# First layer's gates: the modulation weights of each branch consumed in two groups of four, each behind the first half of a gate product

## The chip, the cores and the metric

The kernel runs on one core of one Trainium2 chip. The metric is the device time of one execution in microseconds. Three runs of the kernel before took 3114.62, 3114.74 and 3118.58 us, a median of 3114.74 us. All data are float32.

In this text TensorE is PE, VectorE is DVE, ScalarE is ACT, GpSimd is POOL and SyncE is SP. PE reads its operands from the on-chip memory SBUF and sums in PSUM, which has eight banks of 128 partitions by 512 floats.

## The reference, cut to what matters

The program is a two-layer trunk (attention of three kinds, a Fourier branch, a mixture of 16 experts) followed by a second block of two more layers. What the change touches is the part of the first layer in which the four branches are gated and merged, and the six vectors by which the layer shifts and scales its tokens ("modulation"):

```
def trunk_layer(h_lat, h_ctx, c, c_ctx, w_mod, b_mod, w_in, ...):
    m_lat = (jax.nn.silu(c) @ w_mod + b_mod)[:, None, :]
    m_ctx = jax.nn.silu(c_ctx) @ w_mod + b_mod
    sh1, sc1, g1, sh2, sc2, g2 = jnp.split(m_lat, N_MOD, -1)
    ...
    u_lat = h_lat * (1.0 + sc1) + sh1
    y_lat, y_ctx = token_mixers(u_lat, u_ctx, w_in, ...)
    h_lat = layer_norm(DN_ALPHA * h_lat + g1 * y_lat, ln1_g, ln1_b)

def merge_branches(branches, gate_logits, w_branch, w_out):
    gates = jax.nn.sigmoid(gate_logits)
    merged = gates[..., :D_MODEL] * (branches[0] @ w_branch[0])
    for i in range(1, N_BRANCH):
        merged = merged + gates[..., i * D_MODEL:(i + 1) * D_MODEL] * (branches[i] @ w_branch[i])
    return merged @ w_out
```

The width is 1024; there are 256 latent and 256 context tokens, so 512 columns in the first layer. The gate logits are 4096 of the columns of `u @ w_in`, 1024 for each branch. `w_mod` is 1024 x 6144 for each of the two layers: 12288 columns for a product with only two vectors, `c` and `c_ctx`.

## The kernel before

**The weight stream.** Every large weight is cut into units of 1024 x 256 floats, 1 MB each. The host lays them in one list in the order in which PE uses them (`weight_stream`). SBUF holds a ring of eight units (`ring`). SP refills it (L489): for each unit it waits until the counter `units_used` says that the unit eight places earlier was consumed, and then issues one 1 MB transfer. PE takes units with `unit()`, which waits until the unit has landed (`loaded[n % RING]`). So PE can run at most eight units ahead of a transfer, and a unit is released in list order.

**The modulation product.** `w_mod` of both layers is 48 units in six sets of eight. Two sets are used before the part in question; the other four are used in the first layer's gate stage, one set for each branch. `modulation_rows` multiplies four units at a time: `cs` (the activated `c` and `c_ctx`, padded to 32 columns) is the stationary operand, and each of the four units writes its own 32 partitions of a PSUM bank, so that four units make 32 matmuls of 32 x 256 (L844). Two such groups fill the banks `wb` and `wb + 1`. DVE copies both to SBUF (L2039, L2041, the two tiles of `mrow`), PE transposes them (`modulation_columns`, L852), and DVE adds the bias and writes the vectors `mod` (`columns_of`, L1888).

**The gate stage** (`mix_branches`, on PE, ACT and DVE each). Sixteen chunks of 256 columns run in four slots of four; a slot is a branch, in the order of `ORDER`. In each chunk of the first layer PE issues: the first half of the gate product (L870: 8 matmuls of 128 x 512 into bank `gb`), one step of attention, the second half of the gate product (L870, bank `gb + 1`), another step of attention, and the branch product (L895: 4 matmuls into banks `wb` and `wb + 1`). An attention step `attend(i)` is: transpose the probabilities of pair i (`turn`, L806) in two halves, mix the values of pair i-1 between them (L819), and compute the scores of pair i+1 (L785, with a mask product L790 or L793 for two of the kinds). There are 24 pairs, so the attention ends with chunk 11; chunk 12 mixes the last pair.

On DVE a chunk is: the softmax of pair 2·chunk (L1991 to L2003, with ACT's exponential L1527 in between), then `merge` of the chunk before (L2023 in the first slot; L2026 and L2027 in the others), which frees the banks `wb` and `wb + 1` and counts `merged_step`, then in the first chunk of a slot the work on the modulation rows and columns, then the copy of mixed values (L2012) and the softmax of pair 2·chunk+1. ACT takes the gate's tanh (L1557) and copies the transposed probabilities (L1541).

**In the first chunk of each slot** PE does the whole modulation product before anything else: it waits for `merged_step` (both banks `wb` are still being read by the merge), runs the two groups of four units, and only then takes the gate unit, which is the ninth unit of the list there. After the first half of the gate product it waits for `rows_kept` and transposes the columns.

Below, "the first half of the gate product" is the L870 group with j = 0.

## Time and profile before

| | us |
|---|---|
| median of 3 runs | 3114.74 |
| profiled execution, its own time | 3111.43 |
| its span, first to last instruction | 3109.6 |
| PE busy | 2841.2 |
| DVE busy | 858.0 |
| ACT busy | 347.8 |
| mean DMA rate over the span | 220 GB/s |

The profile is of one execution. A row of the timeline gives where a run of equal instructions starts, how long it lasts, how many there are (a float32 matmul shows as two records, so "x16" is eight matmuls), and in brackets how long the engine had stood idle and what ended that. The gate stage of the first layer lies between 160 and 567 us. The granted clock (PEclk) is the share of TensorE's full speed of 2.4 GHz that was granted: 1.00 is that level, 0.50 is 1.2 GHz throughout a stretch, and values between are stretches with both.

### The profile page before, as it was taken

What the parts mean: (1) busy time and instruction counts of PE and PEld (TensorE: products, weight loads), DVE (VectorE), ACT (ScalarE), POOL (GpSimd) and SP (SyncE); (2) the same over time, 40 slices, a digit from 0 to 9 for tenths busy, and PEclk for the clock granted to TensorE, in tenths of its full rate; (3) what the DMA queues carried; (4) which work ended last, traced back from release to release, by engine and by line L of the source; (5) the groups of instructions that cost most, each with busy time, mean ns of one, the idle gap of its engine ahead of it and who ended that gap; (6) DMA issues with size and microseconds to landing.
All of it is one profiled execution on the core that took longest, in us unless ns stands there. A gap on an engine that the chain in (4) does not pass through costs nothing.

```text
span 3109.6 us, 39609 instructions
## 1 busy us (share of the span) xinstructions
PE 2841.2 (91%) x16504; PEld 2025.8 (65%) x16504; DVE 858.0 (28%) x1787; ACT 347.8 (11%) x710; POOL 52.7 (2%) x92
## 2 busy tenths in 40 slices
PE   7999999998888889999977777899999999998998
PEld 3644444466666667788644343488788887887887
DVE  1322321152222233432311111278622202222201
ACT  0012220020000002121100000011211001011000
POOL 1000000000000001000000000000000000000000
PEclk9999999999999999999998999999999999999999
DMA  8434135149999993233599999933232443342441
GB/s 325 175 143 157 56 157 199 68 157 421 421 420 421 420 411 113 95 107 132 202 415 413 419 418 417 416 140 136 105 122 97 157 144 117 122 142 81 151 148 39
DMA packets 97660, 684.05 MB, mean 220 GB/s; under 512 B 11488, under 2 KB 12640, under 8 KB 16992
## 3 DMA queue, kind: packets, MB, share of 16 engines
q1 hardware_dynamic: 91488, 660.17, 53.7%
q0 software_dynamic: 6016, 21.50, 2.2%
q8 instruction: 135, 2.21, 0.3%
q14 instruction: 21, 0.17, 0.0%
HBM read 678.22 MB, written 3.41 MB: 219 GB/s over the span
## 4 chain that ended last, share of the span: by engine, by line
PE 75%; DMA 19%; DVE 2%; issue 1%; ACT 1%; SPq 1%; ACTq 0%; DVEq 0%
PE ps L605 29%; DMA ring<-units 19%; PE ps L870 11%; PE ps L1032 9%; PE ps L895 3%; PE ps L1337 2%; PE ps L1169 2%; PE ps L623 1%; PE ps L614 1%; PE ps L696 1%; PE ps L692 1%; PE ps L988 1%; PE ps L785 1%; PE ps L916 1%; PE ps L806 1%
## 5 line engine op out<-in xcount | busy, mean ns | idle before, releaser
L1032 PE MATMUL ps<-ring,arena 128*64 128x256 f32 (+1 forms) x4096 | 439.1, 418 | 134.5 <-DMA ring<-units 130.9
L605 PE MATMUL ps<-h,ring 128*128 128x256 f32 (+1 forms) x2176 | 502.6, 393 | 4.9 <-ACT h L1496 4.9
L605 PEld LDWEIGHTS ps<-h,ring 128*128 128x128 f32 x2176 | 413.3, 190 | 92.0 <-issue 37.8
L1032 PEld LDWEIGHTS ps<-ring,arena 128*64 128x64 f32 (+1 forms) x4096 | 287.0, 140 | 274.9 <-issue 187.9
L870 PE MATMUL ps<-u,ring 128*128 128x512 f32 (+1 forms) x1024 | 340.8, 489 | 6.3 <-DMA ring<-units 6.3
L605 PE MATMUL ps<-arena,ring 128*128 128x256 f32 x1408 | 306.6, 379 | 4.7 <-DVE arena L2290 3.4
L605 PEld LDWEIGHTS ps<-arena,ring 128*128 128x128 f32 x1408 | 267.3, 190 | 42.1 <-DVE arena L2290 4.2
L870 PEld LDWEIGHTS ps<-u,ring 128*128 128x128 f32 x1024 | 194.0, 191 | 142.1 <-issue 120.5
L1047 PE MATMUL ps<-ring,arena 128*32 128x256 f32 x2048 | 237.4, 383 | 37.5 <-DMA ring<-units 33.2
L1047 PEld LDWEIGHTS ps<-ring,arena 128*32 128x32 f32 x2048 | 118.0, 109 | 154.5 <-DMA ring<-units 64.7
L2203 DVE COPY u<-ps 32x512 f32<-32x512 f32 (+1 forms) x128 | 70.9, 554 | 245.6 <-PE ps L1032 244.3
L2333 DVE SCALAR_TENSOR_TENSOR arena<-arena,vec 128x256 f32<-128x256 f32 x240 | 97.1, 477 | 0.0
L2227 DVE SCALAR_TENSOR_TENSOR u<-h,ps 128x512 f32<-128x512 f32 x20 | 13.7, 687 | 299.2 <-PE ps L605 299.2
L895 PE MATMUL ps<-arena 128*128 128x512 f32 (+1 forms) x256 | 89.2, 491 | 0.6 <-DVE arena L2012 0.6
L605 PE MATMUL ps<-u,ring 128*128 128x512 f32 (+1 forms) x256 | 85.5, 489 | 2.8 <-DVE u L1851 2.7
L2195 DVE TENSOR_TENSOR arena<-arena,ps 128x256 f32<-128x256 f32 x48 | 20.2, 421 | 239.8 <-PE ps L1032 131.7
L1630 ACT ACTIVATE arena<-ps 128x256 f32<-128x256 f32 x48 | 18.4, 383 | 578.0 <-PE ps L1047 315.3
L2191 DVE SCALAR_TENSOR_TENSOR arena<-arena,ps 128x256 f32<-128x256 f32 x48 | 20.2, 421 | 226.8 <-ACT arena L1630 226.6
L1487 ACT ACTIVATE u<-u 128x512 f32<-128x512 f32 x24 | 14.5, 630 | 590.0 <-DVE u L1821 590.0
L1991 DVE TENSOR_REDUCE small<-ps 128x2 f32<-128x1024 f32 (+1 forms) x36 | 37.7, 1047 | 151.1 <-PE ps L785 76.9
L605 PEld LDWEIGHTS ps<-u,ring 128*128 128x128 f32 x256 | 47.7, 190 | 37.6 <-issue 31.1
L2288 DVE TENSOR_SCALAR arena<-ps 128x512 f32 x32 | 22.1, 692 | 175.6 <-PE ps L605 175.6
(331 smaller groups left out, 2604.8 us busy)
## 6 DMA issues: line engine op xcount, KB each, us to landing
ring<-units SPq DMA_DIRECT2D x624, 1024.0 KB, 12.5
arena<-quarters POOLq DMA_DIRECT2D x32, 256.0 KB, 2.9
h<-tokens SPq DMA_DIRECT2D x1, 2048.0 KB, 26.0
arena<-neighbours POOLq DMA_DIRECT2D x32, 64.0 KB, 5.7
arena<-tokens POOLq DMA_DIRECT2D x1, 2048.0 KB, 8.9
arena<-memory POOLq DMA_DIRECT2D x2, 1024.0 KB, 5.4
con<-constants SPq DMA_DIRECT2D x1, 1712.0 KB, 20.2
early_values<-arena POOLq DMA_DIRECT2D x6, 256.0 KB, 5.2
```

What stands on the lines that cost most here:

```text
L605: last = nc.tensor.matmul(ps[:, g + j, 0:n], w[:, kt, j * P:(j + 1) * P], rhs[:, q * KT + kt, 0:n], start=(q == 0 and kt == 0), stop=(q == ...
L614: last = nc.tensor.matmul(ps[:, g, 0:n], mean, x[:, kt, 0:n], start=(kt == 0), stop=(kt == KT - 1))
L623: last = nc.tensor.matmul(ps[:, g + 1, 0:n], mean, sq[:, kt, 0:n], start=(kt == 0), stop=(kt == KT - 1))
L870: last = nc.tensor.matmul(ps[:, gb + j, 0:T], w[:, kt, j * P:(j + 1) * P], u[:, kt, 0:T], start=(kt == 0), stop=(kt == KT - 1))
L895: last = nc.tensor.matmul(ps[:, wb + j, 0:T], quarter[done % 2][:, kt, j * P:(j + 1) * P], branch[:, 2 * br + kt, 0:T], start=(kt == 0), s ...
L1032: last = nc.tensor.matmul(ps[j * slots:(j + 1) * slots, bank, lo:lo + UC], lhsT[:, kt, 0:slots], w[j][:, kt, :], start=(kt == 0), stop=(kt ...
L1047: last = nc.tensor.matmul(ps[j % 4 * slots:(j % 4 + 1) * slots, banks[j // 4], 0:UC], xcur[:, kt, 0:slots], w[j][:, kt, :], start=(kt == 0 ...
L1169: last = nc.tensor.matmul(ps[:, g + j, 0:S], w[:, kt, j * P:(j + 1) * P], h[:, kt, 0:S], start=(kt == 0), stop=(kt == KT - 1))
L1337: last = nc.tensor.matmul(ps[:, outs[c], j * S:(j + 1) * S], w[:, kt, j * P:(j + 1) * P], mixin[:, q * KT + kt, :], start=(q == 1 and kt = ...
L1991: link(v.tensor_reduce(m, ps[:, sb_:sb_ + 2, lo:512], AX.X, ALU.max))
L2203: last = v.tensor_copy(y4[half][CAP * e4:CAP * (e4 + 1), st, :] .rearrange("p (a j n) -> p a j n", j=beside, n=UC)[:, :, j, :], src.rearra ...
L2333: ins = v.scalar_tensor_tensor(conv[:, t, :], src, k, conv[:, t, :], ALU.mult, ALU.add)
```

## The change

The units, the products and the tiles stay as they are; their order in the list and in the program changes, in the first layer only.

In the list, the eight modulation units of a slot and its first gate units stood as m0 to m7, g0, g1, g2, g3. They now stand as m0 to m3, g0, m4 to m7, g1, g2, g3.

On PE, chunks 0 and 1 of a slot take one group of four modulation units each, after the first half of their gate product (in chunk 0 of the stage also after the scores of pair 0) and before the attention step. The wait for `merged_step` stands before that group and no longer at the start of the slot. Each group uses bank `wb` alone. The transposes of the columns move from chunk 0 to chunk 2 of the slot, behind the first half of its gate product. The branch product of chunks 0 and 1 waits for its copy of the rows, that of chunk 2 for the columns.

On DVE the two row copies stand in chunks 0 and 1, each behind the merge of the chunk before, and `columns_of` stands in chunk 2. ACT computes what it did and counts units in the new order.

```diff
@@ weight_stream
         for b in range(4):
+            gates = w_in[7 + 4 * ORDER[b]:11 + 4 * ORDER[b]]
             if l == 0:
-                parts.append(w_mod[2 + b])
-            parts.append(w_in[7 + 4 * ORDER[b]:11 + 4 * ORDER[b]])
+                parts += [w_mod[2 + b][:4], gates[:1], w_mod[2 + b][4:], gates[1:]]
+            else:
+                parts.append(gates)
@@ PE, mix_branches
-                def modulation_rows(chunk):
+                def modulation_rows(chunk, first):
                     if chunk:
                         pe.wait_ge(merged_step, chunk)
                     else:
                         pe.wait_ge(products_taken, products - 2)
-                    for n in range(2):
-                        w = [unit() for _ in range(4)]
-                        for kt in range(KT):
-                            for q in range(4):
-                                last = nc.tensor.matmul(ps[32 * q:32 * (q + 1), wb + n, 0:UC], cs[:, kt, :], w[q][:, kt, :],
-                                                        start=(kt == 0), stop=(kt == KT - 1))
-                        last.then_inc(units_used, 4)
-
-                def modulation_columns(n):
-                    pe.wait_ge(rows_kept, n + 1)
+                    w = [unit_at(first + q) for q in range(4)]
+                    for kt in range(KT):
+                        for q in range(4):
+                            last = nc.tensor.matmul(ps[32 * q:32 * (q + 1), wb, 0:UC], cs[:, kt, :], w[q][:, kt, :],
+                                                    start=(kt == 0), stop=(kt == KT - 1))
+                    last.then_inc(units_used, 4)
+
+                def modulation_columns(chunk, n):
+                    pe.wait_ge(merged_step, chunk)
+                    pe.wait_ge(rows_kept, 2 * n + 2)
...
-                    if l == 0 and c == 0:
-                        modulation_rows(chunk)
+                    first = state["unit"]
+                    if l == 0 and c < 2:
+                        state["unit"] += 4
                     w = unit()
...
-                                if c == 0:
-                                    modulation_columns(slot)
+                                if c < 2:
+                                    modulation_rows(chunk, first)
+                                if c == 2:
+                                    modulation_columns(chunk, slot)
                                 attend(2 * chunk)
...
-                    if l == 0 and c == 0:
+                    if l == 0 and c < 2:
+                        pe.wait_ge(rows_kept, 2 * slot + c + 1)
+                    if l == 0 and c == 2:
                         pe.wait_ge(columns_kept, slot + 1)
@@ DVE, mix_branches
-                    if l == 0 and chunk % 4 == 0:
+                    if l == 0 and chunk % 4 < 2:
+                        dve.wait_ge(units_used, at(units_used, 4))
+                        v.tensor_copy(mrow[chunk % 4], ps[:, wb, 0:UC]).then_inc(rows_kept, 1)
+                    if l == 0 and chunk % 4 == 2:
                         n = chunk // 4
-                        dve.wait_ge(units_used, at(units_used, 4))
-                        v.tensor_copy(mrow[0], ps[:, wb, 0:UC])
-                        dve.wait_ge(units_used, at(units_used, 4))
-                        v.tensor_copy(mrow[1], ps[:, wb + 1, 0:UC]).then_inc(rows_kept, 1)
                         dve.wait_ge(rows_turned, n + 1)
```

**PE at the start of the stage, chunk 0.** In these rows L844 (L848 in the changed kernel) is the modulation product, L870 (L876) the gate product, L785 (L790) the scores, L852 the column transposes, L806 (L811) the probability transposes. Before:

```order
L844 MATMUL ps<-ring,cond 32x256 [waits unit_loaded_1,unit_loaded_0,unit_loaded_2,unit_loaded_7,products_taken]
L844 MATMUL ps<-ring,cond 32x256 x31
L844 MATMUL ps<-ring,cond 32x256 [waits unit_loaded_5,unit_loaded_6,unit_loaded_4,unit_loaded_3]
L844 MATMUL ps<-ring,cond 32x256 x31
L870 MATMUL ps<-u,ring 128x512 [waits products_taken,unit_loaded_7]
L870 MATMUL ps<-u,ring 128x512 x7
L785 MATMUL ps<-arena 128x512 [waits rotated,products_taken]
L785 MATMUL ps<-arena 128x512
L852 MATMUL ps<-con,arena 128x128 [waits modulation_rows_kept]
L852 MATMUL ps<-con,arena 128x128 x3
L806 MATMUL ps<-con,arena 128x128 [waits probs_ready,products_taken]
```

And in the changed kernel:

```order
L876 MATMUL ps<-u,ring 128x512 [waits products_taken,unit_loaded_3]
L876 MATMUL ps<-u,ring 128x512 x7
L790 MATMUL ps<-arena 128x512 [waits rotated,products_taken]
L790 MATMUL ps<-arena 128x512
L848 MATMUL ps<-ring,cond 32x256 [waits unit_loaded_1,unit_loaded_0,unit_loaded_2,unit_loaded_7,products_taken]
L848 MATMUL ps<-ring,cond 32x256 x31
L811 MATMUL ps<-con,arena 128x128 [waits probs_ready,products_taken]
L811 MATMUL ps<-con,arena 128x128 x3
```

The gate product and the scores moved ahead of the modulation product, of which one group of the two is left here, and the column transposes are gone from the chunk.

**PE at the start of the third slot, chunk 8** (the second and fourth slot read alike). L895 (L905) is the branch product of chunk 7. Before:

```order
L895 MATMUL ps<-arena 128x512 [waits merged_step,quarter_loaded_1]
L895 MATMUL ps<-arena 128x512 x3
L844 MATMUL ps<-ring,cond 32x256 [waits unit_loaded_1,unit_loaded_0,unit_loaded_2,unit_loaded_7,merged_step]
L844 MATMUL ps<-ring,cond 32x256 x31
L844 MATMUL ps<-ring,cond 32x256 [waits unit_loaded_5,unit_loaded_6,unit_loaded_4,unit_loaded_3]
L844 MATMUL ps<-ring,cond 32x256 x31
L870 MATMUL ps<-u,ring 128x512 [waits gate_kept,unit_loaded_7]
L870 MATMUL ps<-u,ring 128x512 x7
L852 MATMUL ps<-con,arena 128x128 [waits modulation_rows_kept]
```

And in the changed kernel:

```order
L905 MATMUL ps<-arena 128x512 [waits merged_step,quarter_loaded_1]
L905 MATMUL ps<-arena 128x512 x3
L876 MATMUL ps<-u,ring 128x512 [waits gate_kept,unit_loaded_3]
L876 MATMUL ps<-u,ring 128x512 x7
L848 MATMUL ps<-ring,cond 32x256 [waits unit_loaded_1,unit_loaded_0,unit_loaded_2,unit_loaded_7,merged_step]
L848 MATMUL ps<-ring,cond 32x256 x31
L811 MATMUL ps<-con,arena 128x128 [waits turned_kept,probs_ready]
```

The gate product now follows the branch product directly and takes the unit of ring place 3, the fifth of the slot, where it took place 7 once more, the ninth; the wait for the merge stands behind it.

**DVE in chunk 8.** L2036 and L2037 are the merge of chunk 7, L2048 the copy of the first group's rows, L2022 the copy of mixed values, L2001 the start of the next softmax, all in the changed kernel:

```order
L2036 SCALAR_TENSOR_TENSOR arena<-arena,ps 128x1024 [waits merged_step,gate_kept,branch_summed]
L2037 TENSOR_TENSOR h<-h,arena 128x1024 [waits dve_step]
L2048 COPY arena<-ps 128x256 [waits units_used]
L2022 COPY arena<-ps 128x2x128 [waits values_mixed]
L2001 TENSOR_REDUCE small<-ps 128x2 [waits scores_ready]
```

The second row copy, which followed the first directly (L2039, L2041), now stands in the same place of chunk 9, and the column work in that of chunk 10.

## Rows read from the trace of the kernel before

**Rows 1.** Page, section 1: busy time of PE and its share.
```profile
PE 2841.2 (91%) x16504; PEld 2025.8 (65%) x16504; DVE 858.0 (28%) x1787; ACT 347.8 (11%) x710; POOL 52.7 (2%) x92
```

**Rows 2.** Chain that ended last, 150 to 510 us: shares by line.
```profile
by line: PE ps L870 50.3%; PE ps L895 9.9%; PE ps L785 5.9%; DMA ring<-units 5.3%; PE ps L806 5.3%; PE ps L844 5.0%; PE ps L819 3.6%; PE ps L752 1.9%; issue 1.8%; ACT arena L1541 1.5%; ACT arena L1527 1.2%; PE ps L790 1.2%; PE ps L793 1.2%;
```

**Rows 3.** PE timeline, chunk 0: start, us, line, count, [idle, releaser].
```profile
159.97 7.11 PE L844 MATMUL ps<-ring,cond 128*32 128x256 f32 x128
168.63 7.13 PE L870 MATMUL ps<-u,ring 128*128 128x512 f32 x16 [1.55 <-DMA ring<-units]
175.69 1.13 PE L785 MATMUL ps<-arena 64*128 64x512 f32 x4
181.96 1.11 PE L852 MATMUL ps<-con,arena 128*128 128x128 f32 x4 [5.13 <-DVE arena L2041]
182.86 1.06 PE L806 MATMUL ps<-con,arena 128*128 128x128 f32 x4
184.61 1.11 PE L806 MATMUL ps<-con,arena 128*128 128x128 f32 x4 [0.69 <-ACT arena L1541]
185.65 2.08 PE L785 MATMUL ps<-arena 64*128 64x512 f32 x4
187.66 8.73 PE L870 MATMUL ps<-u,ring 128*128 128x512 f32 x16
196.23 0.60 PE L806 MATMUL ps<-con,arena 128*128 128x128 f32 x4
196.76 1.09 PE L819 MATMUL ps<-arena 128*64 128x128 f32 x16
197.79 0.66 PE L806 MATMUL ps<-con,arena 128*128 128x128 f32 x4
```

**Rows 4.** PE timeline at the starts of the second, third and fourth slot.
```profile
267.64 3.60 PE L895 MATMUL ps<-arena 128*128 128x512 f32 x8
274.07 7.11 PE L844 MATMUL ps<-ring,cond 128*32 128x256 f32 x128 [2.83 <-DVE h L2023]
282.80 7.13 PE L870 MATMUL ps<-u,ring 128*128 128x512 f32 x16 [1.61 <-DMA ring<-units]
...
381.17 8.80 PE L844 MATMUL ps<-ring,cond 128*32 128x256 f32 x128 [3.42 <-DVE h L2027]
391.58 7.13 PE L870 MATMUL ps<-u,ring 128*128 128x512 f32 x16 [1.60 <-DMA ring<-units]
...
487.00 8.80 PE L844 MATMUL ps<-ring,cond 128*32 128x256 f32 x128 [2.57 <-DVE h L2027]
497.33 7.13 PE L870 MATMUL ps<-u,ring 128*128 128x512 f32 x16 [1.53 <-DMA ring<-units]
```

**Rows 5.** Chain in order of time, start of the second slot: start, us, what.
```profile
277.79 0.05 SPq L489
277.94 4.82 DMA ring<-units
```

**Rows 6.** DVE timeline: softmax and row copy of chunk 0, merge of chunk 7.
```profile
180.01 1.22 DVE L2003 TENSOR_TENSOR arena<-arena,small 128x1024 f32<-128x1024 f32 x1
181.15 0.42 DVE L2039 COPY arena<-ps 128x256 f32<-128x256 f32 x1
...
379.89 1.23 DVE L2027 TENSOR_TENSOR h<-h,arena 128x1024 f32<-128x1024 f32 x1
```

**Rows 7.** Stretches: length, busy PE, PEld, DVE, ACT, POOL; PEclk, DMA share, GB/s.
```profile
182.00:188.00 6.00, 5.31 (x17) 3.08 (x18) 0.98 (x6) 1.19 (x2) 0.00 (x0) 0.50 0.53 221
274.00:282.00 8.00, 7.11 (x128) 4.06 (x128) 0.86 (x3) 0.00 (x0) 0.00 (x0) 1.00 0.36 129
381.00:390.00 9.00, 8.80 (x128) 4.70 (x128) 0.54 (x2) 0.00 (x0) 0.00 (x0) 0.81 0.24 77
398.00:487.00 89.00, 85.80 (x334) 42.19 (x333) 27.18 (x44) 20.30 (x52) 2.15 (x4) 1.00 0.28 108
800.00:900.00 100.00, 85.93 (x727) 61.18 (x724) 23.55 (x51) 5.83 (x15) 0.00 (x0) 1.00 1.01 420
```

More of the change, by code:

```diff
@@ L559, in unit, with unit_at @@
             def unit():
-                n = state["unit"]
+                state["unit"] += 1
+                return unit_at(state["unit"] - 1)
+            def unit_at(n):
                 pe_wait_unit(n)
-                state["unit"] += 1
                 return ring[:, n % RING, :].rearrange("p (k c) -> p k c", c=UC)
@@ L1544, in mix_branches @@
                     done = 16 * l + chunk
-                    if l == 0 and chunk % 4 == 0:
-                        count.skip(units_used, 8)
+                    if l == 0 and chunk % 4 < 2:
+                        count.skip(units_used, 4)
                     if l == 0:
@@ L2035, in mix_branches @@
                         merge(chunk - 1)
-                    if l == 0 and chunk % 4 == 0:
+                    if l == 0 and chunk % 4 < 2:
+                        dve.wait_ge(units_used, at(units_used, 4))
+                        v.tensor_copy(mrow[chunk % 4], ps[:, wb, 0:UC]).then_inc(rows_kept, 1)
+                    if l == 0 and chunk % 4 == 2:
                         n = chunk // 4
-                        dve.wait_ge(units_used, at(units_used, 4))
-                        v.tensor_copy(mrow[0], ps[:, wb, 0:UC])
-                        dve.wait_ge(units_used, at(units_used, 4))
-                        v.tensor_copy(mrow[1], ps[:, wb + 1, 0:UC]).then_inc(rows_kept, 1)
                         dve.wait_ge(rows_turned, n + 1)
```

## The prediction, written before the changed kernel had run

> **What bounds the kernel now.** I read the shares first: PE is busy for 91% of the span [rows 1], so the time goes down only where PE's idle or slow stretches go, and where nothing else makes up for them. Then the chain of work that ended last, cut to the gate stage of the first layer [rows 2]: it is PE nearly throughout, but 5.3% of it is the landing of weight units, and there are shares of ACT and of "issue" besides. Then PE's timeline [rows 3, 4], where one looks for the brackets: a bracket is time in which PE stood idle, and what follows it tells whether the clock fell as well. Between 160 and 505 us there are four places, one at the start of each slot, and each has up to three losses.
>
> The first loss is the wait for the merge: 2.83, 3.42 and 2.57 us before L844 in slots two to four [rows 4]. The branch product of chunk 3 ends at 267.64 + 3.60 = 271.24, and DVE is done with the merge that frees the banks only at 274.0. The second is the wait for the gate unit: 1.55, 1.61, 1.60 and 1.53 us before L870 [rows 3, 4]. That unit stands ninth behind a ring of eight; its transfer can start only when the first group of four is consumed, at 277.79, and takes 4.82 us to land [rows 5], while the second group lasts 7.11 / 2 = 3.6 us. The third is in chunk 0 alone: 5.13 us before L852 [rows 3], because DVE first does the softmax of pair 0 and only then copies the rows [rows 6].
>
> Behind some of these gaps the clock falls. From 182 to 188 us the granted clock was 0.50, which is 1.2 GHz, and L844 of the third slot ran at a mean of 0.81 and took 8.80 us; in the second slot it had 1.00 and took 7.11 [rows 4, 7].
>
> **The change part by part.** No instruction of PE, DVE or ACT is added or taken away: 64 modulation matmuls, 4 transposes and two row copies for each slot stay. Only the places change.
>
> *The merge wait.* PE now goes from the branch product into the first half of the gate product. Its bank is guarded by the gate's tanh of the chunk before, which was issued a whole product earlier, and its unit is the fifth of the slot, so it is in the ring. It lasts 7.1 us, and the merge ends 2.57 to 3.42 us after PE came free, the last at 379.89 + 1.23 = 381.12 [rows 6]. The wait lies under it with 3.7 us to spare. Gone: 2.83 + 3.42 + 2.57 = 8.82 us. Without that cover they would come back in full.
>
> *The unit wait.* The gate unit of chunk 0 of a slot is now in the ring before the slot begins. The next one that could be late is g1, the tenth. Two transfers are ahead of and with it once m0 to m3 are released: the first lands after 4.82 us [rows 5], the next one a unit's time later, 1.05 MB at 420 GB/s, 2.5 us [rows 7]: 7.3 us. PE needs it after an attention step of some 3 us, the second half (7.1), another step (3) and the branch product (3.6 [rows 4]), 17 us in all. So 9.7 us of cover, and m7 has more. Gone: 1.55 + 1.61 + 1.60 + 1.53 = 6.29 us. The refill of the ring, which ran at full rate behind each slot's start, is spread over two chunks; SP's order does not change. The DMA share between the bursts is 0.28 [rows 7], so POOL's 256 KB pieces find room as before.
>
> *Chunk 0.* The scores of pair 0 now end some 8.2 us into the stage instead of at 176.82. The probabilities were written at 181.23, which is 4.4 us after the scores' end [rows 3, 6]. In that time PE now runs one group of rows, 3.6 us, and then waits 0.8 us, with 0.1 us from DVE to PE: 0.9 us. The row copy no longer stands in PE's way, since the transposes come two chunks later. The 0.69 us for ACT's copy between the two halves of `turn` stays. So 5.13 becomes 0.9: 4.2 us.
>
> *The clock.* Behind the gap of 5.13 us five groups ran slow. Against the same groups at full clock [rows 3]: L852 1.11 against 0.60, L806 1.06 against 0.60 and 1.11 against 0.66, L785 2.08 against 1.13, L870 8.73 against 7.13 (7.03 where another L870 is next). That is 0.51 + 0.46 + 0.45 + 0.95 + 1.6 = 4.0 us. L844 of slots three and four lost 8.80 - 7.11 = 1.69 us each, 3.4 in all. With no gap over 0.9 us ahead of them I expect these 7.4 us back: gaps of 0.69 us and below stand in this stage without a fall.
>
> *The cost of more groups.* Rows are now eight groups in eight places, where four pairs stood before; each changes the shape of the stationary operand from 128 columns to 32 and back. The trace of before always has a wait behind L844, so its price is not shown. Its bounds: nothing, as where L819 (64 columns) is followed by L806 at 197.79, while 196.76 + 1.09 is 197.85 [rows 3]; or the tail of one matmul, its 379 ns less the 7110 / 128 = 56 ns at which they follow each other, 0.32 us, for eight groups 2.6 us. I take 0.5 us, near the lower end, because L819 is the nearest row. It could also be a gain of some tenths, since ACT's tanh gets out of the way of its copies in eight chunks.
>
> The Trainium skill speaks against this term: TensorEngine Tiling, "Key Properties", says that changing the tiling mode drains the engine. Taken in full for eight groups that would be the 2.6 us, and the saving 24.1 instead of 26.2 us; the row at 197.79 does not agree, for the mode changes there too and no time is lost.
>
> *What stands behind the changed waits.* On DVE the row copy waits for PE's group, with the copy of mixed values and a softmax queued behind it; both need work that PE issues only after that group, so nobody is held up. In chunk 2 PE waits for `merged_step` behind the first half, which has the same cover of 7.1 us, and the column work is done under the second half. ACT waits in the same order.
>
> *Sum.* 8.82 + 6.29 + 4.2 + 7.4 - 0.5 = 26.2 us. After the stage nothing holds to absolute time: the next units wait in a full ring. The expert stage that follows is bound by transfers (DMA share 1.01, 420 GB/s [rows 7]), but its transfers start when PE releases units, so it begins earlier by the same amount. Against the profiled execution (3111.43, span 3109.6) this gives 3085.2; the median of the three runs lies 3.3 us above that execution, so I forecast 3114.74 - 26.2 = **3088.5 us**.
>
> **The rivals.**
>
> *The clock still falls in chunk 0.* PE has two short gaps there, 0.9 and 0.69 us, with only a 0.6 us transpose between. If that is enough, the 4.0 us are lost again: saving 22.2, time 3092.5. Against it: 2.83 us before L844 of the second slot left the clock at 1.00 [rows 4, 7].
>
> *Only the merge waits and the clock are won.* If a unit wait stays in another place (a transfer longer than I reckon, since other queues share the engines), 6.3 us come back: 3094.8. Against it stands the cover of 9.7 us.
>
> *Nothing arrives at the end.* If the transfers of the expert stage ran on a schedule of their own, PE would only wait longer there: 3114.7. For it: that stage is at 420 GB/s without a break. Against it: from 398 to 487 us the share was 0.28, so the stream was held by the ring and not by its rate. The same time results if the new order is not what runs; the wait for ring place 3 in the changed program speaks against that.
>
> *Slower: the clock drops with each half group.* L844 drives the array with 32 stationary columns, and of three L844 groups behind a gap two took 8.80 us, at 0.81 for the one shown [rows 4, 7]. If each of the eight groups, between small waits, pulled the clock down for what follows as at 182 us, each would cost 4.0 us: 32 us, against 26.2 gained, so 3120.5. It decides from 6.6 falls of that size. For it: two gaps of only 2.57 and 3.42 us were enough, one of 2.83 was not, so the edge is not sharp. Against it: the rows of the second slot ran at 1.00, and in the new order full-array products stand directly ahead of every group. The Trainium skill has a rule of this kind: TensorE: Matmul & The Clock Gate, "A second HAM failure mode: psum-queue depth-cycling", says that short idles between groups of matmuls can make the clock swing between its two levels; the trace agrees only behind gaps of 2.57 us and more.
>
> **How the numbers follow.** Forecast 0.72, clock in chunk 0 0.12, unit wait kept 0.06, nothing arrives 0.06, slower 0.04. The forecast's own spread: the group cost from -0.5 to 2.6, the wait in chunk 0 from 0 to 2, and some 2 us of the medians, which differ by up to 4 us between runs of one kernel (3114.6 to 3118.6): 3083 to 3094. With the two next cases, which reach to 3092.5 and 3094.8, the range is 3083 to 3096. A measurement of this kernel can tell about 0.2% (6.2 us) from no change. Faster by more holds the first three cases, 0.90; within 0.2% the fourth and part of the last, 0.07; slower 0.03.
>
> **What would show it.** In the changed profile: no bracket before the first gate product of slots two to four and none with the ring's DMA between 160 and 500 us; one bracket of about 0.9 us before the first L811 of the stage; granted clock 1.00 from 176 to 196 us and at every L848; the modulation groups 3.6 us each. The stage ends some 26 us earlier, and the time from its end to the end of the span stays what it was. I would be wrong if brackets of over 1 us stood before or behind L848, if the clock rows showed 0.5 to 0.8 in chunks 0 and 1 of the slots, or if the expert stage gained what the gate stage lost.

## The result, and the profile after

The changed kernel took a median of 3089.94 us in four runs (3086.65 to 3092.20), against 3116.66 us for the kernel before in four runs (3114.62 to 3122.79). The ratio is 0.9912 with a 95% interval of 0.9899 to 0.9926: faster by 0.9%. The forecast was 3088.5 us, the range 3083 to 3096.

The first lines of the changed kernel's page, to be held against [rows 1]:

```profile
span 3086.2 us, 39613 instructions
...
PE 2840.0 (92%) x16504; PEld 2020.3 (65%) x16504; DVE 858.1 (28%) x1787; ACT 348.6 (11%) x710; POOL 52.8 (2%) x92
```

The engines do the same work: 1.2 us less of PE over the whole program, 0.1 us more of DVE. The span is 23.4 us shorter. The gate stage by itself, before and then after (the fields are those of [rows 7]):

```profile
159.97:567.33 407.36, 384.69 (x1730) 185.86 (x1730) 103.67 (x187) 73.32 (x186) 8.57 (x16) 0.98 0.36 140
162.88:545.64 382.76, 379.38 (x1729) 182.18 (x1728) 103.87 (x187) 73.99 (x186) 8.59 (x16) 1.00 0.39 149
```

Here PE's idle time fell from 22.67 to 3.38 us, by 19.3 us, and its busy time by 5.3 us. The matmuls are the same, so the 5.3 us are matmuls that ran faster: that is the clock, for the most part. The whole page hides this, since the rest of the program scatters by more.

PE's timeline of the changed kernel in chunk 0, against [rows 3] (start, length, line, count, and in brackets the idle time before):

```profile
162.88 7.03 PE L876 MATMUL ps<-u,ring 128*128 128x512 f32 x16
169.84 1.13 PE L790 MATMUL ps<-arena 64*128 64x512 f32 x4
170.90 3.66 PE L848 MATMUL ps<-ring,cond 128*32 128x256 f32 x64
175.53 0.63 PE L811 MATMUL ps<-con,arena 128*128 128x128 f32 x4 [0.97 <-DVE arena L2013]
176.85 0.66 PE L811 MATMUL ps<-con,arena 128*128 128x128 f32 x4 [0.69 <-ACT arena L1551]
177.43 1.84 PE L790 MATMUL ps<-arena 64*128 64x512 f32 x4
179.21 8.07 PE L876 MATMUL ps<-u,ring 128*128 128x512 f32 x16
```

The wait for the unit and the 5.13 us are gone. What is left are the 0.97 us that the softmax of pair 0 needs beyond one group of rows (0.9 us were forecast) and the 0.69 us for ACT's copy. The two groups behind them are still slow, 1.84 us against 1.13 and 8.07 against 7.13. That was not in the forecast.

The same timeline at the starts of slots two to four, against [rows 4]:

```profile
262.70 3.60 PE L905 MATMUL ps<-arena 128*128 128x512 f32 x8
266.13 7.03 PE L876 MATMUL ps<-u,ring 128*128 128x512 f32 x16
273.09 3.66 PE L848 MATMUL ps<-ring,cond 128*32 128x256 f32 x64
276.68 0.66 PE L811 MATMUL ps<-con,arena 128*128 128x128 f32 x4
...
364.88 3.60 PE L905 MATMUL ps<-arena 128*128 128x512 f32 x8
368.31 7.03 PE L876 MATMUL ps<-u,ring 128*128 128x512 f32 x16
375.27 3.66 PE L848 MATMUL ps<-ring,cond 128*32 128x256 f32 x64
378.86 0.66 PE L811 MATMUL ps<-con,arena 128*128 128x128 f32 x4
...
464.94 3.60 PE L905 MATMUL ps<-arena 128*128 128x512 f32 x8
468.37 7.03 PE L876 MATMUL ps<-u,ring 128*128 128x512 f32 x16
```

No bracket is left before any gate or modulation product. The stretches of the changed kernel (length, busy PE, PEld, DVE, ACT, POOL, granted clock, DMA share, GB/s), against [rows 7]:

```profile
176.00:196.00 20.00, 19.31 (x68) 8.71 (x66) 6.70 (x9) 5.77 (x13) 0.54 (x1) 0.91 0.66 264
273.00:282.00 9.00, 8.84 (x93) 4.98 (x93) 1.95 (x3) 1.79 (x3) 0.00 (x0) 1.00 0.42 162
375.00:384.00 9.00, 8.84 (x92) 4.97 (x92) 1.77 (x3) 1.79 (x3) 0.00 (x0) 1.00 0.45 148
```

The clock is at 1.00 in the stretches shown of slots two and three, and all eight groups of rows took 3.66 us, the length at full clock. In chunk 0 the 0.91 means that part of the stretch ran at 1.2 GHz, where 1.00 was forecast.

**The measure used below** is the length of the gate stage: from the start of its first product (159.97 us before, 162.88 after) to the start of the output product behind it (567.33 before, 545.64 after). That is 407.36 us before and 382.76 us after, 24.60 us less. It is a better measure than the whole time, because the rest of the program scatters. What lies behind the stage took 2542.3 us before and 2540.6 us after; over all eleven profiles of this study it lay between 2540.6 and 2550.2 us, and it did not follow the length of the stage. The 2550.2 is from a second profile of the changed kernel itself. The start of the stage scatters too (159.97 to 163.44 us over the eleven): it came 2.91 us later after the change than before, which is why the spans differ by 23.4 and not by 24.6 us.

### The profile page after: what moved, and what is told of

The parts are those of the page before. It is cut to its first block, busy times and chain, and to the rows that moved or that the text cites. A ratio compares the mean times of both kernels' runs of the same rounds, so it can differ in the third digit from the quotient of the medians.

```text
span 3086.2 us, 39613 instructions
## 1 busy us (share of the span) xinstructions
PE 2840.0 (92%) x16504; PEld 2020.3 (65%) x16504; DVE 858.1 (28%) x1787; ACT 348.6 (11%) x710; POOL 52.8 (2%) x92
## 4 chain that ended last, share of the span: by engine, by line
PE 76%; DMA 19%; DVE 2%; issue 1%; ACT 1%; SPq 1%; ACTq 0%; DVEq 0%
PE ps L610 29%; DMA ring<-units 19%; PE ps L876 11%; PE ps L1042 9%; PE ps L905 3%; PE ps L1347 2%; PE ps L1179 2%; PE ps L628 2%; PE ps L619 1%; PE ps L701 1%; PE ps L697 1%; PE ps L998 1%; PE ps L926 1%; PE ps L790 1%; PE ps L811 1%
## 5 line engine op out<-in xcount | busy, mean ns | idle before, releaser
L876 PE MATMUL ps<-u,ring 128*128 128x512 f32 (+1 forms) x1024 | 340.1, 488 | 0.0
L876 PEld LDWEIGHTS ps<-u,ring 128*128 128x128 f32 x1024 | 194.0, 190 | 134.4 <-issue 120.9
L905 PE MATMUL ps<-arena 128*128 128x512 f32 (+1 forms) x256 | 88.9, 490 | 0.6 <-DVE arena L2022 0.6
L2001 DVE TENSOR_REDUCE small<-ps 128x2 f32<-128x1024 f32 (+1 forms) x36 | 37.7, 1047 | 139.7 <-PE ps L790 65.6
```

Of the source, the lines that this page charges most:

```text
L876: last = nc.tensor.matmul(ps[:, gb + j, 0:T], w[:, kt, j * P:(j + 1) * P], u[:, kt, 0:T], start=(kt == 0), stop=(kt == KT - 1))
L905: last = nc.tensor.matmul(ps[:, wb + j, 0:T], quarter[done % 2][:, kt, j * P:(j + 1) * P], branch[:, 2 * br + kt, 0:T], start=(kt == 0), s ...
L2001: link(v.tensor_reduce(m, ps[:, sb_:sb_ + 2, lo:512], AX.X, ALU.max))
```

## The experiments

I begin with a second set of runs of the changed kernel itself.

**The changed kernel again.**

> The changed kernel itself, as the yardstick for the other two on the same chip, and as a second look at the clock in chunk 0. My theory (whether the clock falls behind gaps as short as 0.97 and 0.69 us, or of 2.6 to 3.5 us, is a draw that differs from execution to execution of the same program): the same brackets to 0.1 us, the stage either 381.3 us (no fall) or up to 383 us (a fall). The rival (the fall belongs to the program): the scores and the gate product behind the two gaps are slow again, 1.84 and 8.07 us, stage 382.8.

It took 3091.95 us (3086.64 to 3098.04), ratio 0.9921 (0.9900 to 0.9943), which is 23.2 us less than the 3115.11 us of the kernel before beside it; the first set had given 26.7. The stage ran from 163.21 to 545.97 us, 382.76 us, the same to 0.01 us. PE's timeline of this run behind the two short gaps:

```profile
175.86 0.63 PE L811 MATMUL ps<-con,arena 128*128 128x128 f32 x4 [0.97 <-DVE arena L2013]
...
177.76 1.73 PE L790 MATMUL ps<-arena 64*128 64x512 f32 x4
179.42 8.18 PE L876 MATMUL ps<-u,ring 128*128 128x512 f32 x16
```

0.60 us and 1.05 us are lost, 1.65 together, as in the first profile (0.71 + 0.94). This favours the rival, that the fall belongs to the program; the next run shows that it isn't quite so.

**The merge wait put back.** On top of the changed kernel:

```diff
                         elif chunk:
                             pe.wait_ge(gate_kept, 2 * done - 1 + j)
+                            if l == 0 and c == 0 and j == 0:
+                                pe.wait_ge(merged_step, chunk)
```

> The changed kernel, with one wait put back: in the first chunk of slots two to four PE waits for the merge ahead of the first half of the gate product, as it did before the change. List, groups and columns stay changed. My theory (the merge wait is worth what its brackets show, and the clock falls with them): brackets of 2.6, 3.4 and 2.8 us come back before the first L870-like group of slots two to four, 8.8 us, and of the clock between 0 and 3.4 us (1.7 us where it falls). The gate stage, 382.8 us in the changed kernel, becomes 391.6 to 395.0 us; the time 3098.5 to 3102. The rival (the wait was hidden by other work and the gain came from the order of the units alone): the stage stays within 2 us of 382.8 and the time near 3090.

It took 3101.92 us (3098.65 to 3108.43), ratio 0.9960 (0.9944 to 0.9975). The stage ran from 160.38 to 552.98 us: 392.60 us, 9.84 more. Its PE timeline in chunk 0 and at the three slot starts:

```profile
173.02 0.63 PE L811 MATMUL ps<-con,arena 128*128 128x128 f32 x4 [0.97 <-DVE arena L2015]
174.34 0.66 PE L811 MATMUL ps<-con,arena 128*128 128x128 f32 x4 [0.69 <-ACT arena L1553]
174.92 1.13 PE L790 MATMUL ps<-arena 64*128 64x512 f32 x4
...
265.05 7.10 PE L878 MATMUL ps<-u,ring 128*128 128x512 f32 x16 [2.92 <-DVE h L2035]
370.98 7.11 PE L878 MATMUL ps<-u,ring 128*128 128x512 f32 x16 [3.51 <-DVE h L2039]
473.94 8.80 PE L878 MATMUL ps<-u,ring 128*128 128x512 f32 x16 [2.67 <-DVE h L2039]
```

The brackets are back, 9.10 us. The merge wait is confirmed, and the order of the units alone is not the gain. Two more things are to be read. In chunk 0, whose program is the changed kernel's, the scores took 1.13 us this time: no fall behind the same two gaps. And at the slot starts the clock fell behind 2.67 us and not behind 3.51. With the clock taken out of both (1.65 us of 382.76; 1.70 of 392.60) the difference is 9.79 us for 9.10 us of brackets: each bracket of this kind costs 0.23 us more than it shows. Groups that follow each other without a wait overlap in the timeline (262.70 + 3.60 is 266.30, and the next starts at 266.13, 0.17 us earlier), and with a wait between them they don't. That accounts for most of the 0.23.

**The unit wait taken away**, on top of the kernel before:

```diff
                         for kt in range(KT):
-                            last = nc.tensor.matmul(ps[:, gb + j, 0:T], w[:, kt, j * P:(j + 1) * P], u[:, kt, 0:T],
+                            early = l == 0 and c == 0 and j == 0
+                            if early and kt == KT - 1:
+                                w = unit()
+                            x = resident if early and kt < KT - 1 else w
+                            last = nc.tensor.matmul(ps[:, gb + j, 0:T], x[:, kt, j * P:(j + 1) * P], u[:, kt, 0:T],
                                                     start=(kt == 0), stop=(kt == KT - 1))
+                            if early and kt == KT - 2:
+                                last.then_inc(units_used, 4)
```

The diff shows PE's gate product alone. The units of the second group are released behind its seventh step and no longer behind the group itself, and DVE's second row copy waits for a counter of its own.

> The kernel before, with the wait for the ninth unit of a slot taken away: the first half of the gate product in the first chunk of each slot multiplies seven of its eight steps by the last modulation unit, which is in the ring already, and takes the gate unit for the eighth alone (this half of four of the 64 gate tiles is therefore computed with other weights). My theory: the brackets of 1.55, 1.61, 1.60 and 1.53 us before the gate product go, 6.3 us, and nothing else moves: gate stage 407.4 - 6.3 = 401.1 us, time some 3110. In chunk 0 the gap of 5.1 us may come out the same. The rival (the wait moves on, to the gate unit at the eighth step or to the next unit): the stage stays at 405 us or more.

It took 3109.17 us (3104.89 to 3113.38, ten runs), ratio 0.9980 (0.9971 to 0.9990). The stage ran from 160.64 to 557.47 us: 396.83 us, 10.53 less than before. PE's timeline:

```profile
181.00 1.11 PE L855 MATMUL ps<-con,arena 128*128 128x128 f32 x4 [5.13 <-DVE arena L2054]
...
186.71 8.16 PE L880 MATMUL ps<-u,ring 128*128 128x512 f32 x16
...
272.54 7.12 PE L844 MATMUL ps<-ring,cond 128*32 128x256 f32 x128 [2.83 <-DVE h L2035]
...
377.97 7.11 PE L844 MATMUL ps<-ring,cond 128*32 128x256 f32 x128 [3.42 <-DVE h L2039]
...
480.44 7.11 PE L844 MATMUL ps<-ring,cond 128*32 128x256 f32 x128 [2.57 <-DVE h L2039]
```

No bracket names the ring's DMA. The 6.3 us are gone and did not move on. The other 4.2 us are the clock for the most part: the merge waits are those of [rows 4] to 0.01 us, and yet L844 took 7.11 us in slots three and four instead of 8.80 (3.4 us), and the gate product of chunk 0 8.16 us instead of 8.73 (0.6 us). The last 0.3 us, 0.07 for each of the four brackets, are the overlap that a wait takes away: L844 and the gate product now overlap by 0.07 us (160.64 + 7.11 is 167.75, the next starts at 167.68).

**The columns of chunk 0 moved back.** On top of the kernel before, on PE (on DVE the column work moves behind the second softmax of the chunk):

```diff
-                                if c == 0:
+                                if c == 0 and slot:
                                     modulation_columns(slot)
...
                     attend(steps * chunk + steps - 1)
+                    if l == 0 and chunk == 0:
+                        modulation_columns(slot)
```

> The kernel before, with one thing moved: in chunk 0 of the stage the column transposes and DVE's column work stand behind the second attention step and the second softmax. The bracket of 5.13 us stood before those transposes and named the row copy. My theory (what is late there is the softmax of pair 0, and the row copy only stands behind it on DVE): the bracket moves to the first probability transpose and is 4.4 us, the clock still falls (4 us), the stage becomes shorter by at most 1 us, 406.4 to 407.4. The rival (the row copy and the columns were the cause): the bracket goes, the clock stays at 1.00, and the stage is shorter by 8 to 9 us, near 398.5.

It took 3120.24 us (3115.45 to 3123.75), ratio 1.0014 (1.0003 to 1.0024). The stage ran from 161.77 to 570.09 us: 408.32 us, 0.96 more than before. PE's timeline in chunk 0, and the start of the second slot:

```profile
183.18 1.09 PE L806 MATMUL ps<-con,arena 128*128 128x128 f32 x4 [4.56 <-DVE arena L2005]
...
186.00 2.08 PE L785 MATMUL ps<-arena 64*128 64x512 f32 x4
...
200.48 3.67 PE L897 MATMUL ps<-arena 128*128 128x512 f32 x8 [1.05 <-DVE small L1861]
...
275.08 8.53 PE L844 MATMUL ps<-ring,cond 128*32 128x256 f32 x128 [2.83 <-DVE h L2025]
```

The bracket moved to the probability transposes and is 4.56 us; the clock fell as before. So the 5.13 us before L852 in [rows 3] named the row copy, but stood for the softmax ahead of it on DVE. The column work turned up as a wait of 1.05 us before the branch product. The expected stage missed that and the fall in the second slot (8.53 us instead of 7.11).

**The scores of pair 0 earlier**, on top of the changed kernel:

```diff
                         for kt in range(KT):
+                            if chunk == 0 and l == 0 and j == 0 and kt == KT // 2:
+                                scores(0)
...
-                            if chunk == 0:
+                            if chunk == 0 and l:
                                 scores(0)
```

> The changed kernel, with the scores of pair 0 in the middle of the first half of chunk 0's gate product, four of eight steps earlier (3.5 us). My theory (the 0.97 us before the first probability transpose is the rest of the softmax that one group of rows does not cover, and the clock fell because of it): the bracket goes, the clock is 1.00 in chunk 0, where it cost 1.7 us, and the stage is 2.7 us shorter, 380.1 us; time 3087. The rival (the clock falls for another reason, such as the 0.69 us gap behind it or what the short transposes do): the bracket goes but the scores and the gate product after it stay slow, and the stage is only 1.0 us shorter, 381.8.

It took 3091.14 us (3086.95 to 3092.80), ratio 0.9917 (0.9900 to 0.9933). The stage ran from 162.07 to 542.37 us: 380.30 us, 2.46 less than the changed kernel, with 2.7 expected. PE's timeline:

```profile
173.88 0.66 PE L811 MATMUL ps<-con,arena 128*128 128x128 f32 x4
175.22 0.65 PE L811 MATMUL ps<-con,arena 128*128 128x128 f32 x4 [0.69 <-ACT arena L1553]
175.81 1.13 PE L790 MATMUL ps<-arena 64*128 64x512 f32 x4
176.87 7.13 PE L878 MATMUL ps<-u,ring 128*128 128x512 f32 x16
```

The bracket of 0.97 us is gone, the clock held behind the one of 0.69. Together they are worth 2.62 us; against it the gate product, now cut in two by the scores, takes 3.53 + 3.63 = 7.16 us from start to start (162.07 to 165.60, 166.66 to 170.29) instead of 6.96 (162.88 to 169.84 in the changed kernel). This is the shortest stage of all, but 2.5 us in 3090 are lost in the scatter of the rest: whether this kernel beats the changed one, these runs can't tell.

**All eight modulation units together**, behind the second half of the gate product (the columns in the second chunk, on DVE both row copies behind the second softmax of the first chunk; the diff shows PE's part):

```diff
-                parts += [w_mod[2 + b][:4], gates[:1], w_mod[2 + b][4:], gates[1:]]
+                parts += [gates[:1], w_mod[2 + b], gates[1:]]
...
                             last.then_inc(units_used, 1)
+                            if l == 0 and c == 0:
+                                modulation_rows(chunk)
                     attend(steps * chunk + steps - 1)
```

> The changed kernel's order without its split: all eight modulation units of a slot are taken in its first chunk, behind the second half of the gate product (list g0, m0 to m7, g1 and on), and the columns in the second chunk. My theory: what matters is that the slot begins with a gate product whose unit is in the ring, not that there are two groups of four; slots two to four are as in the changed kernel, with no bracket before any gate or modulation product. Chunk 0 of the stage is the exception, since there the group of rows covered most of the softmax of pair 0: its bracket before the first probability transpose goes from 0.97 to 4.5 us, and the clock falls behind it (up to 4 us). Stage 384.8 to 388.8 us, against 382.8 in the changed kernel (381.3 without its clock loss). The rival (the split is needed, since the eighth modulation unit or g1 arrives late when all eight are taken at once): brackets of 1 to 2 us on the ring's DMA in all four slots, stage 389 us or more.

It took 3103.03 us (3101.99 to 3109.02), ratio 0.9964 (0.9950 to 0.9978). The stage ran from 163.44 to 559.67 us: 396.23 us, 13.5 more than with two groups. My theory fell for slots two to four and the rival held; only the 4.56 us in chunk 0 came as I had said. PE's timeline:

```profile
176.09 1.09 PE L811 MATMUL ps<-con,arena 128*128 128x128 f32 x4 [4.56 <-DVE arena L2011]
...
193.56 3.66 PE L849 MATMUL ps<-ring,cond 128*32 128x256 f32 x64 [1.52 <-DMA ring<-units]
...
295.54 3.66 PE L849 MATMUL ps<-ring,cond 128*32 128x256 f32 x64 [1.61 <-DMA ring<-units]
...
399.10 3.66 PE L849 MATMUL ps<-ring,cond 128*32 128x256 f32 x64 [1.47 <-DMA ring<-units]
...
498.14 5.35 PE L849 MATMUL ps<-ring,cond 128*32 128x256 f32 x64 [2.24 <-DMA ring<-units]
```

And its chain in chunk 0 (start, length, what):

```profile
188.47 0.05 SPq L491
...
188.62 4.81 DMA ring<-units
```

With g0 first in the list the eighth modulation unit is the ninth of the slot and takes g0's place. Its transfer starts at 188.62, when g0 is released, and lands 4.81 us later; the first group of rows covers 3.66 us of that. It is the wait of [rows 5] with another unit in the part. In the fourth slot the same transfer took 5.52 us (from 492.48), and the wait is 2.24 us.

**The second of the two groups behind the attention step**, on top of the last kernel:

```diff
                             if l == 0 and c == 0:
-                                modulation_rows(chunk)
+                                modulation_rows(chunk, 0)
                     attend(steps * chunk + steps - 1)
+                    if l == 0 and c == 0:
+                        modulation_rows(chunk, 1)
```

> As the kernel with all eight modulation units behind the second half of the gate product, but with the second group of four moved behind the attention step that follows, so that 7 us and not 3.7 lie between the release of the gate unit and the need of the eighth modulation unit (which takes the gate unit's ring place). My theory (the three waits of 1.5 to 1.6 us stood for a transfer of 4.8 us that starts only when the gate unit is released): those waits go in slots one to three and stay in slot four, where no attention is left; in their place PE waits for DVE's row copy before the branch product, 0.7 us each, as slot four showed. Stage 396.2 - 4.6 + 2.2 = 393.8 us, down to 392 without a fall of the clock in slot four. The rival (the ring is short of bandwidth or of order there): the waits stay, stage 396 us.

It took 3100.00 us (3097.91 to 3105.56), ratio 0.9952 (0.9933 to 0.9970). The stage ran from 160.84 to 553.21 us: 392.37 us. PE's timeline in slots two and four:

```profile
299.00 3.67 PE L904 MATMUL ps<-arena 128*128 128x512 f32 x8 [0.75 <-DVE arena L2057]
...
493.36 3.66 PE L848 MATMUL ps<-ring,cond 128*32 128x256 f32 x64 [2.28 <-DMA ring<-units]
```

The unit wait is gone where attention stands between, and stays in the fourth slot, where none is left. Instead PE waits 0.64 to 0.75 us in each slot for DVE's copy of the second rows. So the two groups of the change are worth something beyond the order: each leaves its unit's place long before it is needed, each row copy lies under a gate product, and in chunk 0 the first group covers the softmax.

**The price of a change of shape.** On top of the changed kernel, seven of the eight groups are cut into four pieces, each behind one matmul of the gate product:

```diff
+                            if l == 0 and c < 2 and chunk and j == 0:
...
+                                if kt == KT // 2:
+                                    piece = modulation_rows(chunk, first)
+                                if kt >= KT // 2:
+                                    piece(2 * kt - KT, 2 * kt - KT + 2)
```

> The changed kernel, with the price of a change of shape multiplied: in seven of the eight modulation groups (not the one in chunk 0) the 32 matmuls of 32 stationary columns are issued as four pieces of eight, each behind one 128-column matmul of the second part of the gate product's first half. That is 28 pieces where there were seven, 21 more, and the same matmuls otherwise. My theory (a change of shape costs nothing that can be seen): stage 381.3 to 383 us. The rival (PE drains at each change, 0.32 us a piece as in the upper bound of my prediction, once or twice for each piece): 6.7 to 13.4 us more, stage 388 to 396 us.

It took 3099.03 us (3098.34 to 3104.43), ratio 0.9956 (0.9939 to 0.9972). The stage ran from 162.73 to 552.51 us: 389.78 us, 7.02 more, with no new bracket. My theory fell here as well. PE's timeline of one group:

```profile
193.69 4.45 PE L881 MATMUL ps<-u,ring 128*128 128x512 f32 x10
198.08 1.07 PE L850 MATMUL ps<-ring,cond 128*32 128x256 f32 x16
199.08 1.12 PE L881 MATMUL ps<-u,ring 128*128 128x512 f32 x2
200.14 1.07 PE L850 MATMUL ps<-ring,cond 128*32 128x256 f32 x16
```

A lone gate matmul takes 1.06 us from start to start, where in a run of eight it takes 6.96 / 8 = 0.87 (266.13 to 273.09 in the changed kernel); a piece of a fourth takes 1.00, where a fourth of the 3.59 us of a whole group is 0.90. Nothing stands idle, everything is a little longer. 7.02 / 21 = 0.33 us for each piece.

**Two pieces instead of four.**

```diff
-                                if kt >= KT // 2:
-                                    piece(2 * kt - KT, 2 * kt - KT + 2)
+                                if kt in (KT - 3, KT - 1):
+                                    piece(2 * kt - KT - 2, 2 * kt - KT + 2)
```

> The changed kernel with each of seven modulation groups in two pieces of 16 matmuls instead of one of 32 (four pieces before), with two 128-column matmuls between: 7 more pieces where the run before had 21 more, which cost 7.0 us of stage without any bracket. Theory (each piece costs a fixed 0.33 us for the two changes of shape around it): stage 382.8 + 2.3 = 385.1 us, or 383.5 if the clock does not fall in chunk 0. Rival (what cost 7.0 us was the single gate matmuls between the pieces, each alone, and not the number of pieces): with pairs of gate matmuls the extra is under 1 us, stage 381.5 to 383.5.

It took 3094.26 us (3091.87 to 3098.28), ratio 0.9927 (0.9910 to 0.9943). The stage ran from 163.41 to 548.58 us: 385.17 us, 2.41 more for seven more pieces, 0.34 us each. The price is of the piece, whether one or two gate matmuls stand between. Pieces without a change of shape were not tried, so that the change of shape and not any interruption costs this is not shown by an experiment. The changed kernel's rows speak for it: where the branch product is followed by the gate product, of the same shape, its four matmuls take 3.43 us from start to start (262.70 to 266.13), 0.86 each, no more than in a run of eight.

## Why the prediction was right

The forecast of 26.2 us came out as 24.6 us in the profiled stage, 26.7 us between the medians of the first set and 23.2 us between those of the second. The mechanism is shown best by the stage, and there the sum was 1.6 us too high. That the first medians differ by almost what was forecast is in part luck: what lies before and behind the stage scatters by more than that. Slot by slot, against the brackets and the clock that the prediction added up:

| | lost before, by the rows | gained, by starts in the two timelines |
|---|---|---|
| slot two | 2.83 + 1.61 = 4.44 | 106.52 - 102.18 = 4.34 |
| slot three | 3.42 + 1.60 + 1.69 = 6.71 | 106.67 - 100.06 = 6.61 |
| slot four | 2.57 + 1.53 + 1.69 = 5.79 | 86.50 - 80.70 = 5.80 |
| chunk 0 (slot one) | 1.55 + 4.2 + 4.0 = 9.75 | 107.67 - 99.82 = 7.85 |

The third column has the lengths of the whole slots. A slot runs here from the start of the branch product ahead of it (L895 at 267.64, 374.16 and 480.83 before; L905 at 262.70, 364.88 and 464.94 after) to that of the next; slot one begins with the stage, and slot four ends with it. The idle time alone fell by 19.3 us, and the three waits of the prediction are 8.82 + 6.29 + 4.2 = 19.3 us. So what was off lies in the clock and in the price of the groups.

*The merge wait, 8.82 us.* Right, and shown by putting it back (9.10 us of brackets). The first half of the gate product covers it, since no bracket is left there.

*The unit wait, 6.29 us.* Right, and shown by taking it alone away from the kernel before. The cover that I gave g1 held: no transfer is in any bracket of the changed stage.

*Chunk 0, 4.2 us.* Right: the bracket is 0.97 us. That the softmax and not the row copy was late there is shown by the moved columns (4.56 us) and by the earlier scores (none).

*The clock, 7.4 us.* This is the term whose size was off. In the compared pair 5.7 us came back (2.3 in chunk 0, 3.4 in slots three and four). The rival that the clock still falls in chunk 0 came true by half: 1.65 us were lost, not 4.0. That is the whole of the 1.6 us by which the sum was too high. Two steps were weak. I wrote that gaps of 0.69 us stand in this stage without a fall, but the only gap of that length before, at 184.61 [rows 3], stands inside the slow stretch; of the gaps shorter than 2.5 us only those of 0.16 us and the unit waits of 1.53 to 1.61 us stood without one. And I took one profile's falls as the program's. The three merge waits of 2.6 to 3.5 us occur in four profiles (the kernel before, the merge wait put back, the unit wait taken away, the columns moved), twelve gaps in all: the clock fell behind six of them, behind none of three in one profile and all of three in another. So the 3.4 us of slots three and four are a draw: with a fall behind every second gap, at 1.69 us each, the three slots are worth 2.5 us on average (an estimate). That both falls were in the profile that I had read, and counted in full, was luck. For the gaps of 4.56 and 5.13 us it is no draw: five of five fell. Behind the pair of 0.97 and 0.69 us four of five fell.

*More groups, 0.5 us.* The sum came out, the reason did not. I had read from the row at 197.79 [rows 3] that a change of shape costs nothing. It costs 0.33 us for the way in and out, as the pieces showed, which is nearly my upper bound of 0.32 us. This agrees with the rule that I had set aside (the Trainium skill, TensorEngine Tiling, "Key Properties": a change of mode drains the engine); that it is a drain that takes the time, no run here shows. The timeline does not show the price as idle time, only as starts that lie further apart. In the stage PE's busy time fell by 5.3 us where the clock gave back 5.7, so 0.4 us went to the groups, net. Each slot has one group more that stands by itself, 4 x 0.33 = 1.3 us. Against that, the brackets that went had cost more than they showed: 3 x 0.23 us for the merge waits and 4 x 0.07 us for the unit waits, by the two experiments on them, 1.0 us. That the two nearly cancel is worked out and was not tried by itself, and that my 0.5 us lay so close was luck.

*Nothing arrives at the end, and slower.* Neither. What lies behind the stage took as long as ever; the scatter of 10 us between profiles is not in step with the stage. A fall of the clock with each half group did not occur: all eight groups took 3.66 us.

## What to carry to other kernels

If a ring of N buffers feeds an engine, the work that needs entry N+1 should not stand directly behind the release of the first ones: put an operand that is already in the ring in front, and let each group's release lie a transfer's length ahead of the need. The same product that covers the transfer also covers a wait for a bank that another engine still reads. The bracket names whoever signalled last; what stands ahead of that instruction on its engine may be the real cause, and moving the named one alone shows it. Count a small group between large ones with its price for the changes of shape, and don't add up the slow stretches of a single profile as if each run had them.

## What the runs showed of the hardware that was not expected

- A group of 32-column matmuls between 128-column matmuls costs PE 0.33 to 0.34 us for both changes together (21 more pieces: 7.02 us; 7 more: 2.41 us), with no idle time in the timeline and the clock at 1.00.
- A wait between two groups can cost more than its bracket: three brackets of 9.10 us cost 9.79 us, where the groups on either side overlap by 0.17 us when no wait stands between them.
- The fall of TensorE's granted clock behind a gap is not set by the length of the gap alone: it held behind 3.51, 3.42 and 2.28 us and fell behind 2.57 and 2.24 us. Behind a single gap of 1.47 to 1.72 us (the waits for units in three profiles) it held in all eleven cases, but behind the pair of 0.97 and 0.69 us with a transpose between it fell in four of five; it held in the one case with 0.69 us alone.
- What the fall cost in chunk 0 was 1.65 us in all four profiles where it fell behind the two short gaps, however it was split between the scores and the gate product (0.71 + 0.94 and 0.60 + 1.05 in the changed kernel, 0.42 + 1.23 with four pieces, 0.55 + 1.10 with two). Why the sum is so constant stays open.
